# Token columns of every wide product cut into 512, 512 and 32 in place of three times 352

## The reference

```
h    = rms_norm(x) * (1 + sc1) + sh1            # modulated by the conditioning vector
proj = h @ w_in                                 # 1024 -> 768 + 256 + 32 + 3*512
q    = rms_norm(c_q) @ w_uq ; latent = rms_norm(c_kv) ; k_rope = rope(k_r)
attn = chunk-causal attention over the latent (8 heads; the stream also sees 256 past frames)
conv = 3-tap causal convolution of g_c * u, gated by g_b
x    = x + g1 * (concat(attn, conv) @ w_out)    # 1024 -> 1024
h    = rms_norm(x) * (1 + sc2) + sh2
x    = x + g2 * ((silu(h @ w_gate) * (h @ w_up)) @ w_down)   # 1024 -> 2816 -> 1024
y    = rms_norm(x)
```

## Time and profile before

| | |
|---|---|
| median of 2 runs | 1587.99 us (1587.76 to 1588.23) |
| span of the profiled execution | 1587.3 us, 22404 instructions |
| TensorE busy | 1502.4 us, 95% |
| weight loads busy | 1411.2 us, 89% |
| VectorE busy | 791.1 us, 50% |
| ScalarE busy | 363.7 us, 23% |
| granted TensorE clock, mean over the span | 0.96 of full speed |

### The profile page before, as it was taken

The page is one execution under the profiler, slowest core; times in us unless marked ns, Lnnn a source line. Parts: engine busy times, 40 slices in busy tenths (PEclk is TensorE's granted clock), DMA queues, the critical chain, the costliest instruction groups (busy, mean ns, idle before and its releaser), DMA issues.

```text
span 1587.3 us, 22404 instructions
## 1 busy us (share of the span) xinstructions
PE 1502.4 (95%) x8976; PEld 1411.2 (89%) x8976; DVE 791.1 (50%) x1410; ACT 363.7 (23%) x525; POOL 12.2 (1%) x32
## 2 busy tenths in 40 slices
PE   6899999999799989999699999999999999999997
PEld 6899999998477667679699999999999999999996
DVE  4888788234654737375622424334251433434266
ACT  4421110122143535242521011111111111111116
POOL 0000000001000000000000000000000000000000
PEclk7599999999899999999799999999999999999998
DMA  9244435311100000001011111111111111111102
GB/s 343 74 120 120 119 127 102 114 53 51 63 3 7 0 7 7 13 1 41 26 40 46 49 40 53 42 40 54 41 47 47 41 44 50 40 50 45 41 26 110
DMA packets 109807, 92.88 MB, mean 59 GB/s; under 512 B 8488, under 2 KB 96064, under 8 KB 109728
## 3 DMA queue, kind: packets, MB, share of 16 engines
q1 hardware_dynamic: 109520, 91.63, 18.9%
q10 hardware_dynamic: 208, 0.06, 0.0%
HBM read 85.05 MB, written 6.63 MB: 58 GB/s over the span
## 4 chain that ended last, share of the span: by engine, by line
PE 85%; DVE 8%; ACT 3%; issue 3%; DMA 1%; SPq 0%; DVEq 0%; ACTq 0%
PE PS L530 65%; PE PS L720 4%; PE PS L743 4%; PE PS L649 3%; PE PS L733 2%; PE PS L587 2%; PE PS L704 1%; DVE X L1270 1%; DVE MX L1388 1%; DVE WL L1174 1%; DVE SG L1456 1%; PE PS L637 1%; PE PS L512 1%; ACT HH L873 1%; DMA XR<-in_x_prompt 1%
## 5 line engine op out<-in xcount | busy, mean ns | idle before, releaser
L530 PE MATMUL PS<-H2H,WH 128*128 128x352 f32 x1056 | 341.5, 324 | 13.7 <-DVE H2L L1184 6.9
L530 PE MATMUL PS<-H2L,WH 128*128 128x352 f32 x1056 | 341.5, 324 | 0.0
L1174 DVE TENSOR_TENSOR WL<-RAW,WH 128x1024 fp32r<-128x1024 f32 x95 | 115.8, 1220 | 271.3 <-ACT WH L833 271.1
L530 PE MATMUL PS<-H2H,WL 128*128 128x352 f32 x1056 | 229.0, 325 | 0.0
L530 PEld LDWEIGHTS PS<-H2H,WH 128*128 128x128 f32 x1056 | 200.3, 190 | 15.2 <-issue 11.7
L1270 DVE SCALAR_TENSOR_TENSOR X<-PS,MOD,X 128x32 f32<-128x32 f32 (+5 forms) x312 | 161.9, 577 | 92.6 <-PE PS L530 92.6
L833 ACT ACTIVATE WH<-RAW 128x1024 fp32r<-128x1024 f32 x93 | 98.0, 1055 | 463.2 <-PE PS L530 450.1
L530 PEld LDWEIGHTS PS<-H2L,WH 128*128 128x128 f32 x1056 | 199.8, 189 | 0.0
L530 PEld LDWEIGHTS PS<-H2H,WL 128*128 128x128 f32 x1056 | 181.9, 189 | 0.0
L530 PE MATMUL PS<-AH,WH 128*128 128x352 f32 x528 | 170.9, 324 | 2.7 <-DVE X L1270 2.7
L530 PE MATMUL PS<-HH,WH 128*128 128x352 f32 x504 | 164.4, 327 | 7.2 <-DVE HL L1205 6.6
(11 more groups left out here) (184 smaller groups left out, 1793.6 us busy)
## 6 DMA issues: line engine op xcount, KB each, us to landing
ADA<-in_w_ada SPq DMA_DIRECT2D x16, 1024.0 KB, 5.4
RAW<-in_w_gate SPq DMA_DIRECT2D x22, 512.0 KB, 3.9
RAW<-in_w_up SPq DMA_DIRECT2D x22, 512.0 KB, 3.8
RAW<-in_w_down SPq DMA_DIRECT2D x22, 512.0 KB, 3.7
RAW<-in_w_in SPq DMA_DIRECT2D x20, 512.0 KB, 6.3
ADA<-in_w_ada SPq DMA_DIRECT2D x4, 2048.0 KB, 16.2
XR<-in_x_prompt SPq DMA_DIRECT2D x8, 512.0 KB, 4.7
RAW<-in_w_out SPq DMA_DIRECT2D x8, 512.0 KB, 4.8
```

Source lines behind the costliest of these rows:

```text
L530: mm = pe.matmul(PS[:, b + n, 0:CH], w, x[k][:, n * CH:(n + 1) * CH], start=(first and w is weights[0][k] and x is xs[0]), stop=(last and ...
L1174: dve.tensor_tensor(WL[:, s % 2, :], RAW[:, s % 2, :], WH[:, s % 2, :].bitcast(F32), ALU.subtract)\
```

## The change

The three token chunks are now columns 0 to 511, 512 to 1023 and 1024 to 1055, so that the results of a group lie flat over its three banks: 512 + 512 + 32 columns. The number of matmuls, their order and their stationary tiles stay. The readers now see one flat run of 1056 values; `add_gated` needs two instructions for a group (1024 and 32 tokens, which have different gates) where it had three (704, 320 and 32).

```diff
-CH = T // NCH
+SPANS = ((0, 512), (512, 1024), (1024, T))
...
         def chunks(g, rows=slice(0, P)):
             b = NCH * (g % 2)
-            return PS[rows, b:b + NCH, 0:CH]
+            return PS[rows, b:b + NCH, :].rearrange("p n c -> p (n c)")[:, 0:T]
 
         def in_chunks(ap):
-            return ap.rearrange("p (n c) -> p n c", n=NCH)
+            return ap
 
         def streams(g):
-            b = NCH * (g % 2)
-            return [(PS[:, b:b + 2, 0:CH], slice(0, 2 * CH), 0), (PS[:, b + 2, 0:S - 2 * CH], slice(2 * CH, S), 0),
-                    (PS[:, b + 2, S - 2 * CH:CH], slice(S, T), 1)]
+            return [(chunks(g)[:, 0:S], slice(0, S), 0), (chunks(g)[:, S:T], slice(S, T), 1)]
...
                 for w, xs in ((weights[0][k], moving), (weights[1][k], moving[:1])):
-                    for n in range(NCH):
+                    for n, (lo, hi) in enumerate(SPANS):
                         for x in xs:
-                            mm = pe.matmul(PS[:, b + n, 0:CH], w, x[k][:, n * CH:(n + 1) * CH],
+                            mm = pe.matmul(PS[:, b + n, 0:hi - lo], w, x[k][:, lo:hi],
                                            start=(first and w is weights[0][k] and x is xs[0]),
                                            stop=(last and w is weights[1][k]))
...
             def query_product(j):
                 for k in range(KQ):
-                    for n in range(NCH):
-                        mm = pe.matmul(PS[:, n, 0:CH], WQP[:, k].rearrange("p e d -> p (e d)"),
-                                       CQ[:, k, n * CH:(n + 1) * CH], start=(k == 0), stop=(k == KQ - 1))
+                    for n, (lo, hi) in enumerate(SPANS):
+                        mm = pe.matmul(PS[:, n, 0:hi - lo], WQP[:, k].rearrange("p e d -> p (e d)"),
+                                       CQ[:, k, lo:hi], start=(k == 0), stop=(k == KQ - 1))
```

More of the change, by code:

```diff
@@ L553, in total @@
                 begin_group(g)
-                for n in range(NCH):
-                    mm = pe.matmul(PS[:, NCH * (g % 2) + n, 0:CH], ONES[:], ss[:, n * CH:(n + 1) * CH],
+                for n, (lo, hi) in enumerate(SPANS):
+                    mm = pe.matmul(PS[:, NCH * (g % 2) + n, 0:hi - lo], ONES[:], ss[:, lo:hi],
                                    start=True, stop=True)
@@ L635, in _ @@
                         wait_kept(pe, G_CQ + k)
-                    for n in range(NCH):
-                        mm = pe.matmul(PS[:, NCH * (g % 2) + n, 0:CH],
+                    for n, (lo, hi) in enumerate(SPANS):
+                        mm = pe.matmul(PS[:, NCH * (g % 2) + n, 0:hi - lo],
                                        WQR[:, k, q].rearrange("p h c -> p (h c)"),
-                                       CQ[:, k, n * CH:(n + 1) * CH], start=(k == 0), stop=(k == KQ - 1))
+                                       CQ[:, k, lo:hi], start=(k == 0), stop=(k == KQ - 1))
                 mm.then_inc(ps_full[g % 2], 1)
@@ L1265, in add_gated @@
                     dst = X[:, m, t] if isinstance(m, int) else X[:, bass.ds(m, 1), t].rearrange("p a t -> p (a t)")
-                    if t.start == 0:
-                        dst = dst.rearrange("p (n c) -> p n c", n=2)
                     scalar = MOD[:, gate + m, st:st + 1] if isinstance(m, int) else \
@@ L1375, in _ @@
                     rows = slice(NOPE * e, NOPE * (e + 1))
-                    dve.tensor_tensor(in_chunks(QT[e][rows, :]), PS[rows, 0:NCH, 0:CH], in_chunks(RSQ[rows, :]), ALU.mult)\
+                    dve.tensor_tensor(QT[e][rows, :], chunks(0, rows), RSQ[rows, :], ALU.mult)\
                         .then_inc(q_kept, 1)
```

## The result

The changed kernel takes 1788.08 us (median of 2 runs, 1786.24 to 1789.92) against 1587.99: 1.1258 times as long, with a 95% interval of 1.1237 to 1.128. The span of the profiled execution grew from 1587.3 to 1788.0 us, by 200.7.

What follows compares the result with a forecast made beforehand. TensorE was taken as the bound, each matmul no shorter than the load under it. Line 530 +190, float32 products +6, absorbed waits −2 made +194 on 1587.3, or 1782 us with the median's 0.7; forecast 1755 to 1805 (60%), range 1727 to 1840.

Steps and rivals of the forecast that it cites:

- The narrow matmul costs its load: Line 530: a 32-column matmul takes the 0.111 us of the load under it, not 27.8 ns by its columns.
- loads fetched two ahead: Rival at line 530: loads under earlier wide matmuls make 32-column ones free; 1588 us; 5% together with the 25 ns rule.
- a shorter float32r load: Rival at line 530: load shorter by 46 ns, narrow matmul 65 ns, k step 1.562 us, time 1679; 4%.
- The wide matmul costs 227.8 ns: Line 530: a 512-column float32r matmul takes 66.7 ns more than the 161.1 ns of 352 columns.
- the fixed end: Line 530: the 14.4 ns beyond one cycle per column is fixed per matmul (227.8 ns); growing with columns gives 234.3.
- The rival to which the prediction gave 20%: At line 530 the excess grows with the columns, or comes on top of the load, or both: 1812 to 1840; 20%.
- The rival in which 512 columns carry the small float32 excess: At line 530 the 14.4 ns belongs to 352 columns; 512 take 215.4 ns, k step 1.625 us, about 1727; 8%.
- The float32 products: Lines 637, 649 and 555: a k step grows from 1.775 to 1.936 us, 38 × 0.161 = +6.1 us.
- What is absorbed: Longer k steps first use up TensorE's waits: later HL waits and one group beside the key rotation, about 2 us.
- the additions hide under TensorE: Down groups: 1.7 us of VectorE additions lie under two k steps, 2.90 us before and 3.40 after; saved instruction costed at nothing.
- both excesses together: Line 530: 234.3 ns wide matmuls and 125 ns narrow ones at once, given as the upper bound of 1840.
- the clock falls: Rival: during narrow matmuls the clock drops to 1.2 GHz; a tenth of the k steps there adds some 113 us; 3%.

Runs made afterwards that it cites:

- the bfloat16 pair: Matmuls of the split products read only the upper half of each value as bfloat16: in the kernel before 1549.75 us, in the changed kernel 1572.86 us.
- relief: Kernel before, with ScalarE making the copy AH in the looped part and VectorE's next weight split moved ahead of the AL subtraction: 1581.78 us, ratio 0.996.
- three_reads: Changed kernel with the gated additions cut into three instructions again (704, 320 and 32 tokens): 1788.52 us, ratio 1.1258.
- w400: Kernel before with its tokens cut into 400, 400 and 256 columns, readers using two instructions: 1586.73 us, ratio 0.9996.

## Why the prediction was right, and where its terms were off

1782 was forecast and 1788 measured, by the mechanism named. Step by step:

*The narrow matmul costs its load* (0.111 us). Right: 0.11 between the loads in the timeline after, −200 us for a computed 198 when 1773 of them are left out, and 192 columns that cost no more than 32. The two rivals that made it cheaper, loads fetched two ahead and a shorter float32r load, are refuted. That it is the load and not some other price of a four-byte matmul rests on the loads that stand back to back and on the bfloat16 pair; bfloat16 shortens the load but changes the matmul too, and no run shortened the load alone.

*The wide matmul costs 227.8 ns.* Off: 232.6. The step that failed was the choice of the fixed end, because the float32 rows have a fixed excess. For float32r the excess grows with the columns, 0.446 ns each and 4 ns besides, close to the other end (234.3). The rival to which the prediction gave 20% had this mechanism right, and its time (1812 and more) wrong. The k step gained 0.279 us in place of 0.250, and this term was 760 × 0.279 = +212 where +190 was forecast. The rival in which 512 columns carry the small float32 excess is refuted.

*The float32 products,* forecast +6, measured 1 to 4 by themselves: the query product paid 0.91 us of the 0.97 forecast, and around the second rotary product 1.1 us of waiting and some 1.6 us of lower clock went away. The prediction had neither.

*What is absorbed,* forecast 2, measured 200.7 = 212 + 2 − 13, so 13. The sum left out rows of the table that it was read from: before, the loads waited ten times in feed-forward for gated additions (5.6 us) and four times where the loop begins anew (4.7, of which 1.9 are left), and I had read only the three larger rows. The prediction took it that the additions hide under TensorE, 1.7 us of them in 2.90 us of products. That leaves out what VectorE does just ahead of them at the end of an up product, the burst that relief shortened for a gain of 6 us. The waits went to a longer k step and not to the saved instruction, which was rightly costed at nothing (three_reads). With 1.6 us of lower clock that is 10 of the 13. The rest is net: shorter waits for HL, WL and YL on one side, the two drops of the clock in the convolution stage on the other. It was not taken apart further.

The errors of +22, −4 and −11 partly cancel, which is luck: that the k step grew by more than forecast has nothing to do with how long VectorE's waits had been. The forecast that feed-forward grows by 132 us came close by the same luck (886.1 − 754.1 = 132 for 512 of its 528 k steps): the k steps alone account for 512 × 0.279 = 143, and 11 were absorbed. Two smaller slips changed nothing: sixteen one-column matmuls give 0.106 us each and not 0.105, and both excesses together give 1844 and not 1840 as the upper bound.

The saved instruction cost and gave nothing. The clock was 1.00 in feed-forward, as forecast. The rival *the clock falls* came true for a trace only, in the convolution stage, where the clock was 0.98 in place of 1.00; that was worth some 3 us and not 113. That the narrow matmuls are the reason is not shown: each profile is one execution.

## What to carry to other kernels

A matmul costs the larger of its moving columns and the load that lies under it, the one for the matmul behind it, even when that load brings the tile that is already there. Cut the columns so that no piece is shorter than a load. By the line above that is an estimated 240 columns for the float32r tiles of this kernel ((111.5 − 4)/0.446). Among such cuts with the same number of matmuls the widths did not matter (w400). The floor is read from the distance between loads in the profile, at any place where the columns are too few to cover it. When a bound engine gets slower, look in its table of waits, and in that of its weight loads, for what it will stop waiting for; the small rows count when they are many. When a stretch became faster for no reason of the change, look at the granted clock of both profiles there before you call it a wait.

## What the hardware showed that I had not expected

- At the full clock float32r took 0.446 ns per column between 352 and 512 columns and not one cycle of 0.417, with about 4 ns per matmul. Contiguous two-byte tiles have 150 ns for 352 columns, which is one cycle each and 3 ns; the same halves read from four-byte tiles stand in between (156). At the lower clock the excess was not seen in the trace of before: 352 columns took 0.29 us there (809.06 to 809.35), one cycle of 1.2 GHz each.
- Float32r loads were never closer than 0.11 us to each other at full clock. A bfloat16 load fits into the some 26 ns at which narrow matmuls then follow each other.
- The records of matmuls that wait for a load start up to 0.08 us before they run, so the distance between two such starts (0.03 us in the timeline after) is not what the first of them costs.
